# A stack of five transformer blocks on one core: the first block's modulation dots divided between three engines

## The reference, cut to what matters

```python
c_act = silu(c)                               # 1024 numbers
mod = c_act @ ada_w[i] + ada_b[i]             # 1024 x 6144 weights, 6144 results a block
sh1, sc1, g1, sh2, sc2, g2 = split(mod, 6)
h = rmsnorm(x, gain) * (1 + sc1) + sh1        # into the mixer
x = x + g1 * mixer(h)
h = rmsnorm(x, gain) * (1 + sc2) + sh2        # into the feed-forward network (FFN)
x = x + g2 * swiglu(h)
```

## Time and profile before

| | us |
|---|---|
| median of 3 runs | 1623.74 |
| lowest, highest | 1620.49, 1625.25 |
| the profiled execution, its own time | 1623.93 |
| its span, first to last instruction | 1622.1 |
| granted clock, mean over the span | 0.988 |

### The profile page before, as it was taken

One profiled execution on the slowest core, in us unless ns is written; L12 is line 12 of the kernel. 1 busy time (PEld: TensorE's weight loads), 2 busy tenths in 40 slices (PEclk: granted clock), 3 DMA queues, 4 the chain that ended last, 5 costly groups with the idle time before them and its releaser, 6 DMA issues.

```text
span 1622.1 us, 30800 instructions
## 1 busy us (share of the span) xinstructions
PE 1560.3 (96%) x12496; PEld 1485.1 (92%) x12496; DVE 1193.7 (74%) x1721; ACT 790.7 (49%) x1040; POOL 95.0 (6%) x105
## 2 busy tenths in 40 slices
PE   2989999999999999999999999999999999999998
PEld 1868999999989999999899999789999898899998
DVE  6898877778368777775587776968777777676665
ACT  2555433356354333555543335565333567654543
POOL 0150000001000000011000000220000013200000
PEclk9989999999999999999999999999999999999999
DMA  9855978755256888573478885446878555345550
GB/s 390 345 195 202 381 293 322 279 199 194 91 206 247 340 303 313 223 271 123 179 285 337 306 311 206 148 157 263 345 301 306 209 182 169 126 148 181 181 181 26
DMA packets 54219, 383.74 MB, mean 237 GB/s; under 512 B 6256, under 2 KB 6512, under 8 KB 8448
## 3 DMA queue, kind: packets, MB, share of 16 engines
q1 hardware_dynamic: 50400, 363.75, 59.8%
q0 software_dynamic: 3744, 18.94, 3.3%
HBM read 378.47 MB, written 4.19 MB: 236 GB/s over the span
## 4 chain that ended last, share of the span: by engine, by line
PE 85%; DVE 8%; DMA 3%; ACT 2%; issue 1%; POOL 1%; SPq 0%; DVEq 0%; ACTq 0%
PE PS L1901 71%; PE PS L1922 4%; DVE wlo L1352 3%; DMA CST<-cst_in 1%; PE PS L2045 1%; PE PS L2095 1%; PE PS L1971 1%; DVE adar L1370 1%; DMA adar<-ada 1%; PE PS L2072 1%; ACT whi L944 1%; DVE SCR L1524 1%; DMA raw<-ada 1%; PE PS L1945 1%; PE PS L1935 1%
## 5 line engine op out<-in xcount | busy, mean ns | idle before, releaser
L1901 PE MATMUL PS<-hhi,whi 128*128 128x256 f32 x2496 | 717.7, 288 | 4.8 <-DVE hlo L564 2.4
L1352 DVE TENSOR_TENSOR wlo<-raw,whi 128x2048 fp32r<-128x2048 f32 x234 | 537.0, 2296 | 243.1 <-ACT whi L944 242.5
L1901 PE MATMUL PS<-hlo,whi 128*128 128x256 f32 x2496 | 710.6, 285 | 0.0
L1901 PE MATMUL PS<-hhi,wlo 128*128 128x256 f32 x2496 | 710.3, 285 | 0.0
L944 ACT ACTIVATE whi<-raw 128x2048 fp32r<-128x2048 f32 x234 | 447.1, 1911 | 484.5 <-PE PS L1901 472.3
L1901 PEld LDWEIGHTS PS<-hhi,whi 128*128 128x128 f32 x2496 | 483.6, 194 | 12.5 <-issue 8.8
L1901 PEld LDWEIGHTS PS<-hlo,whi 128*128 128x128 f32 x2496 | 483.9, 194 | 1.3 <-issue 1.2
L1901 PEld LDWEIGHTS PS<-hhi,wlo 128*128 128x128 f32 x2496 | 483.5, 194 | 0.0
L1370 DVE CUSTOM_DVE_ANT_0 adar<-adar,CB 128x1024 f32<-128x1024 f32 x232 | 276.9, 1233 | 11.8 <-DMA adar<-ada 11.8
L1901 PE MATMUL PS<-ahi,whi 128*128 128x256 f32 x968 | 274.5, 284 | 1.1 <-DVE alo L1851 1.1
L1901 PE MATMUL PS<-alo,whi 128*128 128x256 f32 x968 | 273.9, 283 | 0.0
(11 more groups left out here) (225 smaller groups left out, 1325.6 us busy)
## 6 DMA issues: line engine op xcount, KB each, us to landing
raw<-weights SPq DMA_DIRECT2D x234, 1024.0 KB, 6.3
adar<-ada SPq DMA_DIRECT2D x104, 1024.0 KB, 5.8
adar<-ada POOLq DMA_DIRECT2D x12, 1024.0 KB, 5.4
raw<-ada SPq DMA_DIRECT2D x4, 1024.0 KB, 15.1
bias_rows<-acc POOLq DMA_DIRECT2D x12, 256.0 KB, 3.5
adar<-bias_rows POOLq DMA_DIRECT2D x8, 256.0 KB, 3.2
CST<-cst_in SPq DMA_DIRECT2D x1, 1128.0 KB, 22.7
CB<-c_in SPq DMA_DIRECT2D x2, 512.0 KB, 3.9
```

The source lines that it names most:

```text
L1352: v.tensor_tensor(wlo[:, u % CV, :], raw[:, u % RAW, :], whi[:, u % CV, :].bitcast(F32), ALU.subtract).then_inc(lo_done, 1)
L1901: m = pe.matmul(o, w(a), h(b), start=first and k_ == 0, stop=last and k_ == 2, skip_group_check=True)
```

## The change

For units 4 to 9 DVE does the dot of the first block of each half only (`ada_dot` then counts 2). The second block is multiplied by `CB` on POOL, in place (`first_mul`), and ACT then passes over the product with a copy whose accumulator sums the row into `AS` (`first_acc`). A half's next load waits for that sum too; so do `ada_read` and, once, SP ahead of the first FFN loads. `ada_read(5)` to `ada_read(8)` move one unit later in DVE's order, and `ada_sum(9, 1)` from step 2 of the output projection to step 1. The products, loads and sums stand in the orders of POOL and ACT as the diff shows.

```diff
+        ada_mul, ada_acc = sem("ada_second_block_products"), sem("ada_second_block_sums")
         c_in_s, c_act = sem("c_loaded"), sem("c_silu")
         ada_dot, ada_mod = sem("ada_rows_dotted"), sem("ada_ready")
         norm_sq, norm_sum, norm_r = sem("norm_squares"), sem("norm_sums"), sem("norm_roots")
@@ -254,6 +255,10 @@
         has_b2 = "b2" in kinds
         LOOP_ADA = [ADA_UNITS * (l + 1) - (2 if l < 2 else 0) for l in range(L)]
+        def halves_to(a, h):
+            return 2 * (a - 4) + h + 1
         def mixer_ada(l):
@@ -819,6 +824,8 @@
                         for j in range(3):
                             load_unit(f + 2 + 3 * st + j, add=i, more=6 * i)
                         if more:
+                            if l == 0:
+                                sp.wait_ge(ada_acc, halves_to(LOOP_ADA[0] - 1, 1))
                             load_ada(a0 + 2 * i + st)
                 load_unit(f + FFN_UNITS - 1)
                 if more:
@@ -889,30 +896,51 @@
                 def first_ada(a, h):
                     pool.wait_ge(ada_dot, 4 * (a - 1) + 2 * (h + 1))
+                    if a > 4:
+                        pool.wait_ge(ada_acc, halves_to(a - 1, h))
                     pool.dma_start(adar[:, h, :], ada[bass.ds(2 * a + h, 1)].rearrange("a p n -> p (a n)")).then_inc(ada_first[h], 16)
+                def first_mul(a, h):
+                    pool.wait_ge(ada_first[h], 16 * (a - 4) + 16)
+                    w = adar[:, h, D:2 * D]
+                    pool.tensor_tensor(w, w, CB[:], ALU.mult).then_inc(ada_mul, 1)
                 if l == 0:
                     first_ada(4, 0)
                     first_ada(4, 1)
+                    first_mul(4, 0)
+                    first_mul(4, 1)
                     first_ada(5, 0)
                     first_ada(5, 1)
-                    first_ada(6, 0)
+                    first_mul(5, 0)
                 if kind in ("swa", "fox"):
                     for p in range(PAIRS):
                         normalise(p)
                         if l == 0 and p == 1:
+                            first_mul(5, 1)
+                            first_ada(6, 0)
                             first_ada(6, 1)
+                        if l == 0 and p == 2:
+                            first_mul(6, 0)
                         if l == 0 and p == 3:
+                            first_mul(6, 1)
                             first_ada(7, 0)
                             first_ada(7, 1)
                         if l == 0 and p == 4:
+                            first_mul(7, 0)
+                        if l == 0 and p == 5:
+                            first_mul(7, 1)
                             first_ada(8, 0)
-                        if l == 0 and p == 5:
                             first_ada(8, 1)
                         if l == 0 and p == 6:
+                            first_mul(8, 0)
+                        if l == 0 and p == 7:
+                            first_mul(8, 1)
                             first_ada(9, 0)
-                        if l == 0 and p == 7:
                             first_ada(9, 1)
+                            first_mul(9, 0)
+                            first_mul(9, 1)
                 if kind == "b2":
                     bias_load(0)
                     bias_load(1)
@@ -1098,6 +1126,15 @@
                             unit_read(i, KT[:, 2 * (i - 8):2 * (i - 8) + 2, :])
                     gla_act(act, lambda i: hi(u0 + i), gla_read, softmax_set)
+                def first_acc(a, h):
+                    if l:
+                        return
+                    act.wait_ge(ada_mul, halves_to(a, h))
+                    act.wait_ge(ada_mod, a - 1)
+                    w = adar[:, h, D:2 * D]
+                    act.activation(w, w, ACT.Copy, accum_out=AS[:, a % 2, 2 * h + 1:2 * h + 2]).then_inc(ada_acc, 1)
                 if kind == "swa":
                     hi(u0 + 2)
                     if l == 0:
@@ -1111,39 +1148,50 @@
                     rope_read(1)
                     if l == 0:
                         hi(u0 + 3)
+                        first_acc(4, 0)
                         hi(u0 + 4)
+                        first_acc(4, 1)
                     hi(u0 + 5)
                     unit_read(2, V[:, :, 0:UC])
                     rope_read(3)
                     exps(0)
+                    first_acc(5, 0)
                     hi(u0 + 6)
                     exps(1)
                     hi(u0 + 7)
                     probs_copy(0)
                     rope_read(4)
                     exps(2)
+                    first_acc(5, 1)
                     probs_copy(1)
                     rope_read(5)
                     mixed_hi(0)
                     exps(3)
+                    first_acc(6, 0)
                     probs_copy(2)
                     mixed_hi(1)
                     exps(4)
+                    first_acc(6, 1)
                     mixed_hi(2)
                     probs_copy(3)
                     hi(u0 + 8)
                     exps(5)
+                    first_acc(7, 0)
                     mixed_hi(3)
                     probs_copy(4)
                     exps(6)
+                    first_acc(7, 1)
                     mixed_hi(4)
                     probs_copy(5)
                     exps(7)
+                    first_acc(8, 0)
                     mixed_hi(5)
                     probs_copy(6)
                     mixed_hi(6)
+                    first_acc(8, 1)
                     probs_copy(7)
                     mixed_hi(7)
+                    first_acc(9, 0)
                 if kind == "fox":
                     hi(u0 + 2)
@@ -1284,6 +1332,8 @@
                 for i in range(1, OUT_UNITS):
                     hi(plan.uout[l] + i + 2)
                     squares(plan.norm[l] + 1, i - 1)
+                    if i == 1:
+                        first_acc(9, 1)
                 norm(plan.norm[l] + 1, l, 1)
@@ -1363,6 +1413,11 @@
                     v.wait_ge(ada_in[h], 16 * (a - 7))
                 if h == 0 and not (isinstance(a, int) and a < 2):
                     v.wait_ge(ada_mod, a - 1)
+                if isinstance(a, int) and 4 <= a < LOOP_ADA[0]:
+                    w = adar[:, h, 0:D]
+                    v.tensor_tensor_reduce(out=w, in0=w, in1=CB[:], scale=1.0, scalar=0.0, op0=ALU.mult, op1=ALU.add,
+                                           accum_out=AS[:, par_, 2 * h:2 * h + 1]).then_inc(ada_dot, 2)
+                    return
                 for j in range(2):
                     w = adar[:, h, D * j:D * j + D]
                     if isinstance(a, int) and a in (1, 2):
@@ -1373,6 +1428,8 @@
             def ada_add(a, par_, col):
                 v.wait_ge(ada_dot, 4 * a + 4)
+                if isinstance(a, int) and 4 <= a < LOOP_ADA[0]:
+                    v.wait_ge(ada_acc, halves_to(a, 1))
                 v.tensor_tensor(MOD[:, bass.ds(col, 4)], AS[:, par_, :], PAR[:, bass.ds(PAR_AT["ada_b"] + col, 4)], ALU.add).then_inc(ada_mod, 1)
             def ada_all(a):
@@ -1612,14 +1669,13 @@
-                        ada_read(5)
-                        ada_read(6)
+                        ada_read(5)
...
@@ -1628,14 +1684,14 @@
                         ada_sum(7, 1, 1)
                         mask_max(7)
                         recips(6)
-                        ada_read(7)
+                        ada_read(6)
                         ada_sum(8, 0, 0)
                         recips(7)
                         mixed_lo(4)
                         ada_sum(8, 1, 0)
                         mixed_lo(5)
                         mixed_lo(6)
-                        ada_read(8)
+                        ada_read(7)
                         ada_sum(9, 0, 1)
                         mixed_lo(7)
                         lo(u0 + 8)
@@ -1788,8 +1844,10 @@
                 for i in range(OUT_UNITS):
                     if i:
                         lo(plan.uout[l] + i + 2)
+                    if l == 0 and i == 1:
+                        ada_sum(9, 1, 1)
+                        ada_read(8)
                     if l == 0 and i == 2:
-                        ada_sum(9, 1, 1)
                         ada_read(9)
                     if i == OUT_UNITS - 1:
                         add_squares(plan.norm[l] + 1, 4, 5, 3)
```

## The result

| | before | changed |
|---|---|---|
| median, us (4 runs each) | 1623.94 | 1641.71 |
| lowest, highest | 1620.49, 1625.25 | 1641.33, 1648.28 |
| the profiled execution | 1623.93 | 1648.28 |
| ratio | | 1.0115, 95% interval 1.009 to 1.014 |

The change makes the kernel 17.8 us slower. The first part of the changed kernel's profile page: POOL has 26 us more, DVE, which was to be relieved, is busy 3 us longer than before.

A forecast was written before the change was run, and what follows sets the result against it. PE bounds the whole kernel, DVE is the full engine in the first mixer. +3 + (5.4 - 3) + (10.8 - 5.4) + (14.1 - 10.8) + 0 = +14.1 us on 1623.9 gives 1638, range 1629 to 1648.

The forecast's parts named there:

- A dot saved, a product, a sum: Per half in the first mixer: DVE saves 1.15 us, POOL's product takes 2.3, ACT's sum 1.2.
- First stage: First mixer up to the reciprocals of pair 4, five products before them: +3 us, between 0 and 5.75.
- full collision: Up to the reciprocals of pair 4, all five products meet DVE operations, net 1.15 us each: +5.75 us.
- the turns: POOL products and DVE operations with two SBUF inputs exclude each other: 2.3 us lost for 1.15 saved per meeting.
- Second stage: From the reciprocals of pair 4 to the low half of pair 7: late loads raise the delay from +3 to +14.1 us.
- The walk: Step-by-step timing of loads, dots, products and sums for units 7 to 9: delays +5.4, +10.8, then +14.1 us.
- the upper bound: First mixer: 5.75 at first, 2.5 us a product, POOL first at units 7, 8, 9 (6.9): +24.8 us, 1649.
- Late loads: Loads of units 7, 8, 9, issued behind POOL's products, land at 109.4, 125.6 and 139.6, so DVE waits.
- The first, faster one: At POOL's issue of unit 8's load: DVE never waits for loads, some 5 us gained, 1619; 5 in 100.
- Only the turns count: First mixer: loads hide because DVE is late itself, only +3 us remains, 1627; 10 in 100.
- The third: First mixer: POOL wins the ties and PE's longer gaps bring more half clock, +20 to +27, about 1647; 10 in 100.
- Output stage: After the mixer: a dot saved against ACT's sum ahead of a split, 0 us, between -1.2 and +1.5.

The follow-up runs named there:

- With fills: Changed kernel, with POOL's product replaced by two fills of the same 128x1024 block, which only write; 1627.15 us, ratio 1.0011.
- run 6: Changed kernel, with POOL's product waiting until DVE's dot on the same half is done; 1647.06 us, ratio 1.0147.
- Runs 1 to 4: Second blocks left out of the kernel before, 1612.85 us; that with the change's load order, 1618.55; changed kernel with 8-column products, 1623.31; with two fills per product, 1627.15.
- the ceiling: Kernel before, with the second block of each half of units 4 to 9 left out altogether; 1612.85 us, ratio 0.9924.
- run 5: Changed kernel, with the second block's product made by DVE right behind its dot instead of by POOL; 1635.18 us, ratio 1.005.
- experiment 3: Changed kernel, with POOL multiplying only 8 of the 1024 columns, all waits and orders kept; 1623.31 us, ratio 0.9984.

## Why the prediction was right, and where not

It gave 1638 us in a range of 1629 to 1648; 1641.7 was measured. By the median it is 3.7 us short, by the marker 5.7 (+19.8 for +14.1). That the median came closer is in part luck: the next mixer, behind the marker, moves by more than the 2.0 us between the two.

- **Place and sign.** Right: the whole effect is in the first mixer and its output stage, and but for the next mixer's own scatter it is carried unchanged to the end. The first FFN dot, forecast at 171 to 172, came at 177.42.
- **A dot saved, a product, a sum.** 1.15, 2.3 and 1.2 us were taken; 2.34 for a product alone, and 1.05 and the accumulator's 0.19 for ACT's sum, hold.
- **First stage, mis-sized.** Forecast +3, measured +6.6 (110.89 for 104.29), beyond the 5.75 of "full collision". With fills these reciprocals come at 98.91, 5.4 earlier than before, so the dots saved are worth what the forecast took (5.75), and the turns cost 12.0 where +3 leaves them 8.75. The bound counted 2.3 lost and 1.15 saved for each product; but DVE and PE also wait for each other: with the rotation at 63.70 stretched, PE's wait before the first scores grew from 1.7 to 4.3 us, and at 80.52 DVE waits 1.7 us for PE, where before it did not. The forecast also left out a sixth product, that of (4, first) at 50.20. It does stretch a dot, to 3.43 us, but DVE's wait of 3.31 us behind it shrinks to 2.12 and takes most of that up.
- **Second stage, the ties.** The walk let DVE go first wherever dot and product wait for one landing. POOL went first (56.15, 129.84, 143.56, and at 112.26 with a normalising instruction ahead of it), as in the upper bound. But that bound's 6.9 us for three ties is too much: from the reciprocals of pair 4 to the low half of pair 7 the delay grew by 13.6 us, where the forecast had 11.1 and the bound 19. At units 7 and 8 a product that goes first also lets the next load go out sooner; only at unit 9, with no load of the mixer behind it, is the whole 2.1 us to be seen. In run 6, where DVE went first, the low half of pair 7 was 1.6 us earlier and the loads were no earlier.
- **Late loads.** Here the walk was good. Between the first loads of units 7, 8 and 9 it had 16.2 and 14.0 us; measured are 17.1 and 14.4, and before 10.1 and 10.4. DVE's new idle was forecast at 2, 7 and 6 us before units 7, 8 and 9; it was 1.1, 5.4 and 4.3. "This is the larger part" holds for the place, 13.6 of 20.2 us. It does not hold for the cause: with fills the loads stand in the same order and are 13.9 and 11.0 us apart, and nothing is lost at the marker. About 3 us of each round are thus turns and the product's extra length, and these the forecast booked under late loads.
- **The sum in another order.** Runs 1 to 4 give steps of the marker from the ceiling: loads' order +2.8, sums and their waits +4.2, POOL's time of 1.95 us +2.7, together 9.7, as much as freeing DVE brings (152.17 to 142.52). POOL's reading against DVE's: +19.5 to 19.8, with 0.39 us of length a product in it. Taken in another order the steps would differ: in run 5, where DVE is not relieved, the same late loads and sums cost 8.4.
- **Rivals.** The first, faster one, set as its condition that POOL is done with (7, second) by 109.4. In experiment 3 the first load of unit 8 goes out at 109.31, and DVE still waits 5.0 us for it, because it comes earlier itself; the ratio, 0.9984, is nearly no change, not 5 us faster. "Only the turns count" was priced at +3 and given 1 in 10. Run 5 is against it, since late loads cost by themselves; but the turns it names are worth six times its price. The third, POOL wins the ties and PE's clock falls, at +20 to +27, has the ties right and the clock (0.80 from 110 to 127 for 0.84), and its lower end is nearer to the marker's +19.8 than the forecast is.
- **Output stage.** Set to 0. The low half of pair 7 was 20.2 late, the marker 19.8: -0.4.
- **The miss, added up.** +3.6 in the first stage, +2.5 in the second and -0.4 in the output stage make the 5.7 by which the marker missed. PE's clock has no term in it.

The steps rest on single profiles of each kernel; the changed kernel's two profiles differ by 0.3 us at the marker. What the low clock costs behind the first stage is not separated: no run holds the clock.

## What to carry to other kernels

Before work goes from DVE to POOL, ask what DVE runs meanwhile: if its operations read two tensors from SBUF, a POOL instruction that reads SBUF can be added to DVE's time whole. Here 21 of 28 us were, for 13.8 saved. So 2.3 us of POOL for 1.15 us of DVE was a loss where DVE was the full engine. Test it with a fill in place of the product: it keeps POOL's time and drops the turns. And where a tile is a ring of load, use and reload, price the move by when the next load can go out, not by the engine's busy time. When an experiment moves the end, look where in the stretch it does so: run 6 gained 5.3 us in one stage and lost more in the two others, and its end alone told the opposite of its first half.

## What the runs showed of the hardware

- A POOL fill of 128x1024 takes 0.95 us and takes no turn with DVE's dots (12 dots in 14.71 us beside 24 fills); a POOL product of the same size takes 2.34 us and does (12 dots in 28.99 us). The Trainium skill ("SBUF — State Buffer", section "Who interferes with whom") says so of instructions that only write; the runs agree.
- Where POOL's product and DVE's dot waited for the same landing, POOL began first each time, by about 0.05 us (56.08 and 56.15, 129.79 and 129.84, 143.51 and 143.56; the same three in the second profile).
- A DVE dot that waits is not sure of the next turn. At 112.26 it waited through POOL's instruction of 112.20 and through the one of 113.20 as well (4.38 us). POOL waits in turn: a product that begins during a split of DVE's took 4.07 us (147.66).
- A mixer in which PE is never idle took 99.1 to 105.2 us for the same instructions, at granted clocks of 0.98 to 0.92. Times of single executions of this kernel differ by more than many changes are worth (before: 1620.4 to 1630.3 over all runs).
